# An unread fp32r product of 32 columns ahead of each gate tile's projection

## The reference, cut to what matters

```python
SEQ, D_MODEL, DEPTH = 512, 1024, 2
PEER_HEADS, PEER_TOPK, N_KEYS = 8, 16, 128         # 16384 experts

for l in range(DEPTH):
    mod = cond @ ada_w[l] + ada_b[l]
    h = modulate(rms_norm(x, mix_norm_g[l]), sh1, sc1)
    x = x + g1 * token_mixer(h, ...)               # SSD scan, pooling, stick-breaking attention
    h = modulate(rms_norm(x, ffn_norm_g[l]), sh2, sc2)
    x = x + g2 * peer_ffn(h, ...)                  # the stage that the change touches

def peer_ffn(h, w_q, keys, u_tab, v_tab):
    # the top 16 experts of each token and head, and their softmax gates
    act = einsum('thkd,td->thk', u_tab[experts], h)
    coef = gates * gelu(act)
    return einsum('thk,thkd->td', coef, v_tab[experts])
```

## Time and profile before

| | us |
|---|---|
| median of 3 runs (2833.16 to 2835.15) | 2833.22 |
| the profiled execution, its own time | 2834.17 |
| span of its profile, first to last instruction | 2832.4 |
| TensorE matmuls busy | 2785.6 (98%) |
| VectorE busy | 2493.2 (88%) |
| ScalarE busy | 1387.9 (49%) |
| GpSimd busy | 952.5 (34%) |
| granted TensorE clock, mean | 0.999 |

### The profile page before, as it was taken

How to read it: one execution, slowest core, us unless ns; L and a number is a source line. 1 busy time by engine, 2 the same in 40 slices (tenths; PEclk the granted TensorE clock), 3 DMA queues, 4 the chain that set the end, 5 groups by cost and what they waited for, 6 DMA issues and landing times.

```text
span 2832.4 us, 49104 instructions
## 1 busy us (share of the span) xinstructions
PE 2785.6 (98%) x17864; PEld 2590.7 (91%) x17864; DVE 2493.2 (88%) x5020; ACT 1387.9 (49%) x2321; POOL 952.5 (34%) x773
## 2 busy tenths in 40 slices
PE   7999999999999999999999999999999999999998
PEld 4767789999999999999988788999999999999998
DVE  4667789999999799999987679999999979999998
ACT  3345225477777433333353532445777753333333
POOL 1000018833335244444400000694333434434342
PEclk9999999999999999999999999999999999999999
DMA  7434648999999899999932122699999999999996
GB/s 276 181 119 178 246 157 305 352 337 399 389 382 348 335 387 384 393 390 392 395 119 75 60 74 83 223 345 334 391 386 393 362 335 365 383 386 382 396 387 251
DMA packets 257144, 855.06 MB, mean 302 GB/s; under 512 B 26080, under 2 KB 59104, under 8 KB 250336
## 3 DMA queue, kind: packets, MB, share of 16 engines
q1 hardware_dynamic: 149280, 442.23, 42.1%
q0 software_dynamic: 98496, 381.73, 35.7%
q10 hardware_dynamic: 9216, 29.36, 2.6%
HBM read 777.06 MB, written 76.15 MB: 301 GB/s over the span
## 4 chain that ended last, share of the span: by engine, by line
PE 66%; DVE 19%; DMA 7%; issue 4%; ACT 3%; POOL 1%; SPq 0%; DVEq 0%; ACTq 0%; POOLq 0%
PE banks L1099 32%; PE banks L1636 8%; PE banks L1633 8%; PE banks L1640 8%; DMA w_raw<-wst 5%; PE banks L1597 3%; DVE w_lo L1680 2%; DVE stages L2180 2%; DVE vacc L2192 2%; PE banks L1434 2%; PE banks L1171 1%; ACT w_hi L811 1%; DVE pick L2300 1%; DVE pick L2304 1%; DMA pj<-adaw 1%
## 5 line engine op out<-in xcount | busy, mean ns | idle before, releaser
L811 ACT ACTIVATE w_hi<-w_raw 128x1024 fp32r<-128x1024 f32 x596 | 628.4, 1055 | 632.2 <-PE banks L1099 322.6
L1680 DVE TENSOR_TENSOR w_lo<-w_raw,w_hi 128x1024 fp32r<-128x1024 f32 x522 | 637.8, 1222 | 236.5 <-ACT w_hi L811 192.1
L769 POOL DMA_INDIRECT ring<-v,gidx x320 | 394.1, 1232 | 610.6 <-DVE vacc L2192 520.4
L1099 PE MATMUL banks<-hH,w_hi 128*128 128x352 f32 (+1 forms) x2528 | 513.4, 345 | 2.0 <-ACT act_out L1025 2.0
L1099 PE MATMUL banks<-hH,w_lo 128*128 128x352 f32 (+1 forms) x2528 | 492.2, 336 | 3.2 <-POOL w_lo L756 1.6
L1099 PE MATMUL banks<-hL,w_hi 128*128 128x352 f32 (+1 forms) x2528 | 490.9, 336 | 0.0
L1099 PEld LDWEIGHTS banks<-hH,w_hi 128*128 128x128 f32 x2528 | 415.7, 188 | 39.5 <-issue 11.0
L1099 PEld LDWEIGHTS banks<-hH,w_lo 128*128 128x128 f32 x2528 | 427.0, 188 | 24.9 <-POOL w_lo L756 3.7
L1099 PEld LDWEIGHTS banks<-hL,w_hi 128*128 128x128 f32 x2528 | 427.6, 188 | 19.0
L769 POOL DMA_INDIRECT ring<-u,gidx x244 | 281.8, 1155 | 455.0 <-DVE gact L2180 444.3
L2192 DVE SCALAR_TENSOR_TENSOR vacc<-ring,gcoef,vacc 128x1024 f32<-128x1024 f32 x316 | 404.2, 1279 | 7.1
(11 more groups left out here) (354 smaller groups left out, 3895.9 us busy)
## 6 DMA issues: line engine op xcount, KB each, us to landing
w_raw<-wst SPq DMA_DIRECT2D x596, 512.0 KB, 6.6
activations<-act_out SPq DMA_DIRECT2D x124, 352.0 KB, 8.0
act_in<-activations SPq DMA_DIRECT2D x62, 704.0 KB, 7.3
gate_matrices<-stages ACTq DMA_DIRECT2D x64, 448.0 KB, 7.8
gates<-gate_matrices SPq DMA_DIRECT2D x64, 448.0 KB, 8.9
ada_buf<-adaw POOLq DMA_DIRECT2D x24, 1024.0 KB, 6.9
nrm<-adaw POOLq DMA_DIRECT2D x8, 1024.0 KB, 5.2
pj<-adaw POOLq DMA_DIRECT2D x7, 1024.0 KB, 7.1
```

Source lines behind the costliest of these rows:

```text
L769: pool.indirect_dma_start(out=gather_slot(l, k), out_offset=None, in_=rows[:, :], in_offset=bass.IndirectOffsetOnAxis(ap=gidx[:, k % UG:k ...
L811: nc.scalar.activation(w_hi[g % 2][:, :, :].rearrange("p a b -> p (a b)"), w_raw[:, g % RAWS, :], ACT.Copy).then_inc(s_wh, 1)
L1099: last = mm(bank[s][:, 0:t.stop - t.start], a[s][:, k, :], b[:, k, t], start=(k == 0 and a is w_hi and b is hH), stop=(k == KT - 1 and a i ...
L1680: v.tensor_tensor(w_lo[g % 2][:, :, :].rearrange("p a b -> p (a b)"), w_raw[:, g % RAWS, :], w_hi[g % 2][:, :, :].rearrange("p a b -> p (a ...
```

## The change

`project` gets an argument `doubled`. Where it is set, the tile begins, behind its two waits, with one more product: the weights of its first true product (`w_hi`, k = 0) with the first 32 of the 352 columns of `hH`, into the first 32 columns of its own bank. Nothing reads it: the true first product starts its accumulation anew and overwrites these columns. The tiles 42 to 119 of both layers set it to 32, the others leave it out.

```diff
-            def project(l, n, s, tokens=None):
+            def project(l, n, s, tokens=None, doubled=0):
...
                 pe.wait_ge(s_wh, l * STREAM + n + 1)
                 pe.wait_ge(s_taken, l * TAKEN + n + 1)
+                if doubled:
+                    mm(bank[s][:, 0:doubled], w_hi[s][:, 0, :], hH[:, 0, t.start:t.start + doubled], start=True, stop=True)
                 for a, b in ((w_hi, hH), (w_hi, hL), (w_lo, hH)):
...
-                def u_tile(n, s):
-                    project(l, U0 + n, s, tokens=slice(TG, T))
+                def u_tile(n, s, doubled=0):
+                    project(l, U0 + n, s, tokens=slice(TG, T), doubled=doubled)
...
                     for j in range(tiles):
-                        u_tile(i * GATE_LOOP + (GATE0 + j), j % 2)
+                        u_tile(i * GATE_LOOP + (GATE0 + j), j % 2, 32)
...
                 for n in range(GATE0 + loops * GATE_LOOP, GATE1):
-                    u_tile(n, n % 2)
+                    u_tile(n, n % 2, 32)
```

## The result

The kernel with the unread product takes 2854.61 us (median of 6 runs, 2850.44 to 2860.16), the kernel before 2833.52 beside it (6 runs, 2832.99 to 2837.76): a ratio of 1.0071, interval 1.0058 to 1.0084. It is **slower**, by 21.1 us or 0.7%. The profiled execution took 2855.66, its span is 2853.7 us, 21.3 more than before.

The account below looks back on a forecast made before the run. The prediction took the gate stretches as bound by TensorE, with VectorE and the DMA engines close behind. It summed 17.3 - 12.9 - 0.9 - 0.8 = +2.7 us, giving 2835.9, say 2836, range 2826 to 2851.

Parts of the forecast that it names:

- The load step: At each gate tile's start, the new product's weight load is exposed: 156 x 0.111 = +17.3 us.
- Rows 7 and 8: Trace rows of short fp32r products: loads start 0.11 us apart, and the first long product behind needs 0.29 us.
- The pace: Gate tiles at 380 or 400 cycles per product: all become short, -12.9 us; bounds nothing to +13.9 us.
- that side: The bad side of the 16-cycle grid, where short and long gate tiles supposedly enter one or two cycles apart, alternating.
- The grid of 16 cycles: Estimate that the start of a product stream is held against 16-cycle steps, which sets a tile's pace at entry.
- The tally of 8 of 11 entries: Behind short fp32 products, first eight products took 1.51 or 1.52 us in 8 tiles, 1.56 in 3; taken as favouring short.
- That the alternation ends: Short and long gate tiles stop taking turns and the 75 long ones become short, 75 x 0.172 = -12.9 us.
- the -0.9 of the forecast: Short gate tiles might be 0.012 us shorter, 1.9 us if all are; half was taken.
- The tail: Tiles 120 to 127 of layer 0 would be entered at 380 cycles: 1.6 us at most, half taken, -0.8.
- What is hidden: In the gate stretches, other engines and queues keep their cover; interruptions may move: 0, with 2 us either way.
- All tiles long: Rival: every gate tile goes at 400 cycles, 17.3 + 13.9 = +31 us, 2864.5; chance 0.09.
- the mixture: Rival: the gate tiles' pace changes at each interruption, total about 2843 us; chance 0.07.

Follow-up runs that it names:

- narrow: Kernel after, with the unread product loading 32 weight columns instead of 128 and writing 32 partitions: 2831.71 us, ratio 0.9986; repeated, 2830.01 us, 0.9989.
- two: Kernel after, with two unread 32-column products ahead of each gate tile instead of one: 2849.08 us, ratio 1.005 to the kernel before.
- cols128: Kernel after, with 128 columns in the unread product instead of 32: 2834.91 us, ratio 0.9997 to the kernel before.
- const: Kernel after, with the constant neg_ge as both weights and moving columns of the unread product: 2834.41 us, ratio 0.9996 to the kernel before.
- mconst: Kernel after, with the unread product keeping the tile's first weights but reading 32 constant columns of neg_ge: 2832.37 us, ratio 0.9997 to the kernel before.
- cols64: Kernel after, with 64 columns in the unread product instead of 32: 2833.2 us, ratio 0.9999 to the kernel before.
- from224: Kernel after, with the unread product's 32 columns of hH read from column 224 instead of 160: 2848.04 us, ratio 1.0056 to the kernel before.
- end96: Kernel after, with the unread product's 32 columns of hH read 96 columns further on, from column 256: 2833.68 us, ratio 1.0004 to the kernel before.
- from192: Kernel after, with the unread product's 32 columns of hH read from column 192 instead of 160: 2832.82 us, ratio 1.0 to the kernel before.

## Why the prediction was wrong, point by point

- **The load step: right.** +17.3 was forecast, 156 x 0.1115 = +17.4 measured; the first true step stayed at 0.246, where the earlier trace rows had 0.25. Rows 7 and 8 gave it. The Trainium skill (TensorE: Matmul & The Clock Gate, Back-to-back issue gap) gives 25 ns for a product without its load; no 32-column product here went at that. narrow, two and cols128 show that the load sets the step and not the columns: a quarter of the weight columns, half the time; a second product, the same again; 96 more columns, nothing in the sum of the first two steps.
- **The pace: wrong, and this is the step that failed.** The prediction put it: "A shift by 267 = 16 x 16 + 11 cycles takes both entries away from that side", and took -12.9 us for it. Measured: +9.5, since 140 of 156 tiles are long and none is thrown back. Two errors lie in it. The grid of 16 cycles was no bad guess (eight periods bear it out), but a shift that is counted in rounded durations can't tell where on it an entry lands: I argued from rows with 10 ns, 24 cycles, and even at the 1 ns of the records the first two steps don't separate the paces. The working had a wrong term as well: a bf16 group isn't 67 x 16 cycles to the next tile but 0.430 us, 1032 cycles or 64.5 x 16, since the next product starts 0.028 us behind the last of the group, half a step of the others. And I treated the entry as a thing of durations alone, while const and mconst have the same load step as the kernel after, 0.111 or 0.112 us, and differ from it only in what is read. The tally of 8 of 11 entries was no evidence either: those come once each, behind fp32 products, while a gate tile is entered from the cycle that the tile before it left, so one outcome repeats 78 times. The fair reading was that the pace would be one of the closed cycles; nothing in the rows of before chose between all long and all short.
- **That the alternation ends: right**, in all sixteen kernels with an unread product, that of the change among them. Twelve went short throughout or nearly, three long, and one each way in a layer. The size of the term, 75 x 0.172 us, was right where it happened: cols64 pays the same load step, and 17.2 - 12.9 less 1.9 for short tiles of 3.892 in place of 3.904 us (the -0.9 of the forecast) is +2.4; it shows +0.3 in its stretches, with 2.1 us fewer hold-ups for the rest. So the forecast of +2.7 describes cols64 (2833.2 beside 2833.38) and not the change.
- **The tail: right in sign, too small, and wrong in reason.** -0.8 was forecast, -3.3 measured. Both tails run at 380 cycles, 30.50 us for eight tiles. That of the kernel before in layer 1 (32.21) I had read as 380 cycles and waits for stores. It was so for four tiles; the other four are at 400, and one wait stands among them (timeline of TensorE, kernel before):

```profile
2305.58 1.43 PE L1099 MATMUL banks<-hH,w_lo 128*128 128x352 f32 x8
2306.84 1.50 PE L1099 MATMUL banks<-hH,w_hi 128*128 128x352 f32 x8
...
2315.66 1.60 PE L1099 MATMUL banks<-hH,w_hi 128*128 128x352 f32 x8 [0.65 <-ACT act_out L1025]
```

  At 2306.84 the pace changes with no idle time of TensorE and no other product between. So the sentence of the prediction that a pace, once begun, stays until something else comes between is wrong too.
- **What is hidden: right.** VectorE's busy time in the stretches is as before, the clock is 1.00, and the hold-ups changed by -1.2 us, within the 2 us that I kept for them.
- **The chances.** "All tiles long" stood there with its price, 2864.5, and 0.09; the mixture with 2843 and 0.07. What came is the first with its tails and with the 16 short tiles of layer 1: 701.8 + 17.2 + 13.9 = 732.9 would be all long at the lengths of before; 727.3 is measured, with 16 short tiles (-2.8), tiles 0.011 and 0.008 us shorter than before (-1.6) and the hold-ups (-1.2). The range ended at 2851 because the tally of 8 against 3 had made that rival cheap.
- **What stays open**: why the repeating sequences close on 16 cycles, why the place of the first columns read, within 256 bytes, goes with the pace for 32 columns and no more for 64, what changed the pace at 2306.84, and what decides which cycle a stretch takes in an execution (layer 0 and layer 1 of from224). The base address of `hH` isn't in the profile, so only differences between places are known.

## What to carry to other kernels

A stream of equal products with something short between has several paces, and the sequence mostly falls into one that repeats; a change of nothing but the columns that the short product reads was worth 20 us in 2800 here (2854.61 in the kernel after, 2833.68 in end96). So price an inserted instruction by its load step from a row, but don't forecast a gain or a loss from the pace: put both closed cycles into the range, and count long and short tiles in the profile before explaining a difference by the work that was added. Where a kernel's runs spread more than those of the kernel before, look by stretch whether one executes at two paces.

## What the runs showed of the hardware that wasn't expected

- The periods of all eight repeating sequences looked at here are whole multiples of 16 cycles of 2.4 GHz, and the 352-column fp32r product has two paces, 380 and 400 cycles, kept for up to 78 tiles, but once left amid a stream without a wait (2306.84 in the kernel before).
- The place of the columns read by a 32-column product (128 bytes more or less) goes with the pace, with equal weights, shape and destination: all twenty runs of end96 and from192 lie between 2828.57 and 2835.78 us, the six of the kernel after from 2850.44 up. At one place both paces occur in one execution, 350.96 and 364.65 us for a gate stretch (from224).
- More work can take less time: the gate stretches 720.7 us with two unread products against 727.3 with one, and 702 with one of 64 or 128 columns.
- A bf16 product with 32 weight columns and 32 columns costs 0.25 us between full-width ones, five times one with 128 of both (0.05), while an fp32r product of the same small size costs 0.056. Only one such kernel ran; why is open.
